# The weight tiles move to 64 bytes past a multiple of 128; every other tile stays where it is

## The reference

```
x = x + stick_breaking_mixer(rmsnorm(x))   # 16 heads: w_qkv, w_o
x = x + relu(rmsnorm(x) @ w1)**2 @ w2      # 1024 -> 4096 -> 1024
x = x + hgrn2_mixer(rmsnorm(x))            # 8 heads, 128 x 128 states: w_in, w_o
x = x + relu(rmsnorm(x) @ w1)**2 @ w2
```

## Time and profile before

| | |
|---|---|
| median of 3 runs | 1958.53 us (1958.06 to 1961.35) |
| the profiled execution | 1954.92 us |
| its span, first to last instruction | 1953.1 us |
| PE busy | 1915.3 us, 98% |
| PEld busy | 1614.7 us, 83% |
| DVE, ACT, POOL busy | 54%, 41%, 56% |
| mean granted clock of TensorE | 0.995 |
| bytes read from HBM | 155.91 MB |

### The profile page before, as it was taken

One profiled execution on the slowest core, in us unless ns is written; L12 is line 12 of the kernel. 1 busy time (PEld: TensorE's weight loads), 2 busy tenths in 40 slices (PEclk: granted clock), 3 DMA queues, 4 the chain that ended last, 5 costly groups with the idle time before them and its releaser, 6 DMA issues.

```text
span 1953.1 us, 28792 instructions
## 1 busy us (share of the span) xinstructions
PE 1915.3 (98%) x10808; PEld 1614.7 (83%) x10808; DVE 1062.0 (54%) x1911; ACT 810.5 (41%) x1378; POOL 1084.6 (56%) x1321
## 2 busy tenths in 40 slices
PE   7999999999999999999999999999999999999998
PEld 5878777888888877778888888878888888888887
DVE  5548774622224467676755555474645476555552
ACT  4455344533333455564533444432222254344441
POOL 5327333455557433316788888643333268888882
PEclk9999999999999999999999999999999999999999
DMA  5214222133333211213333323321221133232331
GB/s 175 68 33 120 54 55 65 50 81 97 97 108 108 77 54 55 61 38 89 94 98 93 103 87 96 120 76 56 65 65 55 44 98 97 87 108 87 91 110 59
DMA packets 269164, 159.87 MB, mean 82 GB/s; under 512 B 6137, under 2 KB 267489, under 8 KB 269026
## 3 DMA queue, kind: packets, MB, share of 16 engines
q1 hardware_dynamic: 269026, 158.02, 27.8%
HBM read 155.91 MB, written 2.10 MB: 81 GB/s over the span
## 4 chain that ended last, share of the span: by engine, by line
PE 86%; DVE 7%; ACT 2%; issue 2%; POOL 2%; DMA 1%; SPq 0%; DVEq 0%; ACTq 0%
PE bank L251 15%; PE bank L1991 12%; PE bank L615 7%; PE bank L616 7%; PE bank L617 7%; PE bank L2631 3%; PE bank L2666 3%; PE bank L2633 3%; PE bank L1592 3%; PE bank L2632 3%; PE bank L417 2%; PE bank L1594 2%; PE bank L1593 2%; PE bank L419 2%; PE bank L418 2%
## 5 line engine op out<-in xcount | busy, mean ns | idle before, releaser
L233 POOL TENSOR_TENSOR weight_lo<-weight_stage,weight_hi 128x256 fp32r<-128x256 f32 x1160 | 961.8, 862 | 778.0 <-ACT weight_hi L221 777.9
L221 ACT ACTIVATE weight_hi<-weight_stage 128x1024 fp32r<-128x1024 f32 (+2 forms) x303 | 309.0, 1021 | 261.9 <-PE bank L251 173.0
L251 PE MATMUL bank<-hidden_hi,weight_lo 128*128 128x512 f32 x512 | 201.4, 393 | 8.9 <-DVE x_t L2342 4.5
L615 PE MATMUL bank<-a_hi,weight_lo 128*128 128x512 f32 (+1 forms) x464 | 198.0, 427 | 2.2 <-DVE a_lo_rounded L1129 1.6
L251 PE MATMUL bank<-hidden_lo,weight_hi 128*128 128x512 f32 x512 | 199.5, 390 | 0.0
L251 PE MATMUL bank<-hidden_hi,weight_hi 128*128 128x512 f32 x512 | 199.4, 389 | 0.0
L617 PE MATMUL bank<-a_hi,weight_hi 128*128 128x512 f32 (+1 forms) x464 | 182.3, 393 | 0.0
L616 PE MATMUL bank<-a_lo_rounded,weight_hi 128*128 128x512 f32 (+1 forms) x464 | 182.2, 393 | 0.0
L1967 POOL TENSOR_TENSOR block_weight_lo<-block_weight,block_weight_hi 128x256 fp32r<-128x256 f32 x156 | 124.1, 825 | 62.2 <-ACT block_weight_hi L2125 62.2
L2342 DVE TENSOR_TENSOR x_t<-x_t,bank 128x512 f32<-128x512 f32 x128 | 81.3, 680 | 101.5 <-PE bank L251 101.0
L251 PEld LDWEIGHTS bank<-hidden_hi,weight_lo 128*128 128x128 f32 x512 | 96.1, 188 | 34.6 <-issue 14.2
(11 more groups left out here) (383 smaller groups left out, 4412.2 us busy)
## 6 DMA issues: line engine op xcount, KB each, us to landing
weight_stage<-in_mlp_w SPq DMA_DIRECT2D x128, 512.0 KB, 3.7
weight_stage<-in_w_in SPq DMA_DIRECT2D x57, 512.0 KB, 3.7
weight_stage<-in_hg_w_in SPq DMA_DIRECT2D x32, 512.0 KB, 3.8
weight_stage<-in_sb_w_qkv SPq DMA_DIRECT2D x24, 512.0 KB, 3.5
weight_stage<-in_w_mkv SPq DMA_DIRECT2D x8, 512.0 KB, 3.7
weight_stage<-in_w_out SPq DMA_DIRECT2D x8, 512.0 KB, 4.1
weight_stage<-in_sb_w_o SPq DMA_DIRECT2D x8, 512.0 KB, 3.7
weight_stage<-in_hg_w_o SPq DMA_DIRECT2D x8, 512.0 KB, 3.6
```

The lines of the kernel that those rows point to most:

```text
L221: act.activation(self.hi[slot][:, 0:size], self.stage[slot][:, 0:size], ACT.Copy).then_inc(self.hi_done, 1)
L233: last = pool.tensor_tensor(self.lo[slot][:, part], self.stage[slot][:, part], self.hi[slot][:, part].bitcast(F32), ALU.subtract)
L251: last = pe.matmul(out, l, r, start=n == 0, stop=n == 3 * len(pairs) - 1)
L615: pe.matmul(to, wlo, ahi(k), start=k == 0, stop=False)
```

## The change

The gap ahead of the ring shrinks by 64 bytes, and a new tile of 64 bytes, never read or written, follows the ring. The ring's twelve tiles so start at 16832 + 4096 n, which is 64 bytes past a multiple of 128 and 192 past a multiple of 256. x_t still starts at 66048, and so every other tile keeps its address. No instruction is added, removed or moved; the operands of those that touch the ring have another start address.

```diff
-FIRST_GAP, SECOND_GAP = 96, 80
+FIRST_GAP, HALF_LINE, SECOND_GAP = 80, 16, 80
...
         S.sb("large_tiles_at_512", [P, FIRST_GAP], F32)
         S.W = Weights(nc, S.sb, S.sem, w)
+        S.sb("half_line", [P, HALF_LINE], F32)
```

## The result

The changed kernel takes 1962.88 us at the median of 13 executions (1956.34 to 1966.86); the kernel before, on the same chips, 1957.93 us at the median of 13 (1952.22 to 1961.35). The ratio is 1.0023, with a 95% interval of 1.0012 to 1.0034. It is slower by 5 us, 0.23% by the ratio: an unchanged time lies outside the interval, and the size is near the 0.2% that the prediction took as what can be told of this kernel. The forecast was 1958.5, no change; the range of 1941 to 1979 holds the time, the forecast's own of 1955 to 1962 just misses it.

The account below looks back on a forecast made before the run. The prediction took PE to bound the kernel, as number of matmuls times step; load, pair, ACT, POOL and DMA, each 0, added to 1958.53 gave 1958.5 us, its own range 1955 to 1962, over the cases 1941 to 1979.

Parts of the forecast that it names:

- the term of the pair: PE's weight load running beside the moving columns, in products reading the ring: 0 at the new address, bounds -14 to +50 us.
- PE hardly stands for the ring: PE's waits for ring tiles: the longest entry of that kind is 1.4 us in two waits at L615.
- 3500 wide steps were put down as settled: Of 5544 ring products 512 columns wide, 3500 estimated to run at 227 ns a step, the others at 231.
- the 1961 worked out from the Trainium skill: DMA writes into the ring: 22 beats for 16, so the first load 2.6 us later and the sum 1961.
- Never settled: Rival: all wide ring products on PE run at 231 to 232 ns; +16 us, 1974; chance 0.24.
- Out of each other's way: Rival: the offset parts PE's two streams; 1944 at the shortest step, 1866 if the whole surplus falls; chance 0.24.
- The supply is late: Rival: POOL or the DMA is slower, PE waits on `weight_lo`; +2 to +5 us, 1962; chance 0.04.
- Every pair worse: Rival: each PE load begins mid-line and needs one line more; up to +50 us, 2008; chance 0.08.
- The control: At L1991 the products on the unmoved block weights must stay at 283, whatever those on the ring do.

Follow-up runs that it names:

- e13: Against the kernel before, the ring starts 160 bytes before a multiple of 512, the moving tiles untouched; ratio 1.0142.
- e1: Against the kernel before, every tile, ring and moving tiles alike, starts 64 bytes earlier; 1958.05 us, ratio 1.0001.
- e2: Against the kernel before, the ring stays at multiples of 512 and every tile behind it starts 64 bytes later; 1961.42 us, ratio 1.0025.
- e3: Against the kernel before, weight_hi and weight_lo alone start 64 bytes before a multiple of 512, weight_stage stays at multiples of 512; 1965.70 us, ratio 1.0051.
- e9: Against the kernel before, only the block weights move, to 64 bytes before a multiple of 512; 1955.94 us, ratio 0.9997.
- e7: Against the kernel before, only the block weights move, to 64 bytes past a multiple of 512; 1955.16 us, ratio 0.9988.
- e11: Against the kernel before, the ring stays at multiples of 512 and everything behind it starts 448 bytes later; ratio 1.0110.

## Why the prediction was wrong

**The step that failed** is the term of the pair: "a shift of the start by 16 columns should change only the ends. The value is the least certain of the sum", taken as 0. It is +7.1 us for the wide and -5.9 for the narrow products, and by the narrow ones' earlier end +3.3 us of waiting for the split: +4.5 us in all. The conclusion from "within one load the two pass each other at every distance" is refuted by the table: if it held, all its rows would be alike. The bounds for the term, -14 and +50 us, held for every distance tried (e13 is the worst, 28 us above before). The waits were misread as well: PE stood for the split at the start of twelve MLP rounds already in before, under the name "issue", and so an early PE could not keep its gain. "PE hardly stands for the ring" left these out, and a wait on POOL that the sum has at 0 came to 3.3 us, though POOL was no slower. That 1958.5 is only 4 us off is luck: two changes of 7.1 and 5.9 us, both taken as nothing, nearly cancel.

**What was right.** That the pair of streams is what the address acts on, and not one of them: e1 and e2 show it, by moving both or the other. The load's own record does not change: for the moved `weight_lo` at L417 it is 187 to 188 ns in both traces. 3500 wide steps were put down as settled; 3566 of 5075 are, by the start times (steps of 226 or 227 ns where nothing waits). ACT's 616 ns stay. POOL's split takes 716 ns at the least and 743 at the median, against 713 and 742. The DMA landing lengthened (3.7 to 3.8 for the MLPs' units, 3.7 to 3.9 for the first block's) and cost nothing that the time of e1 shows, where all the ring's tiles lie as in the change; nor do POOL and ACT by their own speed. So the 1961 worked out from the Trainium skill (DMA: Bandwidth & Descriptors, How a descriptor splits into AXI transactions) is near the time by accident only: of the six beats more for sixteen, 38%, the landing shows 3 to 5%. And what the Trainium skill has under SBUF — State Buffer, Who interferes with whom, two independent ports for PE's two streams, does not hold here as a statement on the step: every row of the table but the first two disagrees. Whether the streams meet in SBUF or inside PE no run tells.

**The rivals.** "Never settled" was nearest: in after no long stretch keeps to steps of 226 and 227 ns. Its price was mis-sized. It put all wide steps at 231 to 232 ns, as in the earlier trace rows, for +4.5 ns on 3500. But those rows are of broken streams. And it turned records into steps by taking off 162 ns, which gave 226 for a record of 388; the step is 228.9. A long stream after the change finds a cycle of its own, 226, 229 and 232 ns in turn, with a mean of 229.0: +2.3 ns on 3566, 8.2 us. The products of hgrn2 that were unsettled stay so; the timeline of after, to be read against the earlier trace rows:

```profile
1404.85 0.40 PE L2632 MATMUL bank<-a_lo_rounded,weight_hi 128*128 128x512 f32 x1
...
1406.69 1.00 PE L2666 MATMUL bank<-hg_q,hg_k 128*128 128x64 f32 x8
```

Eight steps in 1.84 us, 1.85 before. "Out of each other's way" was right for the narrow products alone, whose gain the prediction took from the wide ones' spread; 119.9 to 115.7 ns took back 5.9 of the 7.1 us, and the wait for the split gave 3.3 of these up again. A fall by the whole surplus, 13.3 ns, was hardly open to the narrow ones: the loads of `kpe_sq` in before, with next to no moving columns, follow each other at 112 ns by their starts, and the most frequent narrow step at -64 is 113. That the two widths could move in opposite directions was in no rival. "The supply is late" had the right wait, of PE on `weight_lo`, with a wrong reason. "Every pair worse" is what the distances -32, -96, 128, +32, +64 and +96 do, but for the narrow half. Had the change been by one of these, 1.0074 to 1.0142, the forecast would have been wrong by three to six times as much. A slower supply is excluded by e2 and e3.

**The control worked.** The prediction named the block weights at L1991 as the products that must stay at 283. They did while those beside them went to 278, which pointed to the address before any experiment.

## What to carry over

When a kernel is bound by matmuls back to back, the starts of the weight tile and the moving tile relative to each other, modulo 256 bytes, are a parameter like a tile size: keep both at the same offset for 512 columns (here, with 128 x 128 weights in fp32r, any other distance tried costs 0.2 to 1.4%), and measure a step by first and last start over a long unbroken stretch, not by the mean record. A shift of everything together by 64 bytes was free. A step that gets shorter is worth its sum only where the operand is there earlier as well; look for the split or copy that finishes just in time.

## What was not expected of the hardware

- With 128 x 128 weights changed at every product and the clock at 2.4 GHz, 512 moving columns step at 226.7 to 234.3 ns in the long stretch of L417 and 256 columns at 114.3 to 119.9 on the mean, as the distance of the two start addresses changes. 213.3 and 106.7 ns are 512 and 256 cycles of 2.4 GHz; at 1.2 GHz, where 256 columns step at 0.21 us, nothing comes on top.
- The period is 256 bytes, the smallest shift tried (32 bytes) already costs 6.7 ns a wide step, and the sign counts (-64: 228.9 ns, +64: 233.3).
- The step isn't constant within a stretch but a short cycle: 226 and 227 ns at distance 0, 226, 229 and 232 at -64. What in SBUF or PE makes the cycle stays open; the runs show the dependence, not its mechanism.
- The optimum differs by width: of the distances tried 0 for 512 columns, -64 for 256.
- The distance isn't all for the narrow step: at -64 the block products step at 114.3 ns (e9) and the ring's at 115.7 (after); at +64 they step at 117.7 (e7) and 116.9 (e11). The 2 to 4 ns above are larger, but the rest stays open.
